# Two transformer stacks on one core: attention scores of several heads interleaved on TensorE

## The reference

```python
s = jnp.einsum('bnqkgd,bnjkd->bnkgqj', qb, kband).astype(jnp.float32) * (d ** -0.5)      # B
m = jnp.maximum(s.max(axis=-1, keepdims=True), sink)
p = jnp.exp(s - m)
denom = p.sum(axis=-1, keepdims=True) + jnp.exp(sink - m)
o = jnp.einsum('bnkgqj,bnjkd->bnqkgd', (p / denom).astype(v.dtype), vband)
...
s = jnp.einsum('bqhcd,bkhcd->bhcqk', qq, k).astype(jnp.float32) * scale                  # C
a = (p[:, :, 0] - lam * p[:, :, 1]).astype(v.dtype)
...
q = jnp.concatenate([q[..., :MLA_NOPE], rope(q[..., MLA_NOPE:], positions)], -1) * (dqk ** -0.5)
k = jnp.concatenate([k_nope, jnp.broadcast_to(k_pe, (B, S, H, MLA_ROPE))], -1)           # MLA
s = jnp.einsum('bhqd,bkhd->bhqk', qi, k, preferred_element_type=jnp.float32)
```

## Time and profile before

| | |
|---|---|
| median of 3 runs | 2145.54 us (2145.14 to 2146.28) |
| profiled execution | 2144.2 us, its span 2142.0 us |
| mean granted TensorE clock | 0.998 |
| VectorE busy, ScalarE busy | 65%, 49% |
| chain that ended last | PE 91%, DVE 4% of the span |
| DMA | 377.95 MB, 176 GB/s on average |

### The profile page before, as it was taken

How to read it: one execution, slowest core, us unless ns; L and a number is a source line. 1 busy time by engine, 2 the same in 40 slices (tenths; PEclk the granted TensorE clock), 3 DMA queues, 4 the chain that set the end, 5 groups by cost and what they waited for, 6 DMA issues and landing times.

```text
span 2142.0 us, 31461 instructions
## 1 busy us (share of the span) xinstructions
PE 2104.0 (98%) x13601; PEld 1902.0 (89%) x13607; DVE 1393.6 (65%) x1480; ACT 1059.8 (49%) x1240; POOL 142.1 (7%) x80
## 2 busy tenths in 40 slices
PE   7999999999999999999999999999999999999998
PEld 6998899899989989888998988998789989888997
DVE  5868777785867666566645786556775566566554
ACT  4655555555555544454544665445554443454442
POOL 2001110020101004000000000000000005000000
PEclk9999999999999999999999999999999999999999
DMA  7534565473355555555655645655356555455653
GB/s 250 179 113 137 192 204 179 162 226 119 133 179 181 189 185 179 172 172 177 199 186 171 202 167 187 204 189 146 128 172 209 187 185 193 157 174 171 207 190 106
DMA packets 252930, 377.95 MB, mean 176 GB/s; under 512 B 14085, under 2 KB 195578, under 8 KB 252794
## 3 DMA queue, kind: packets, MB, share of 16 engines
q1 hardware_dynamic: 252506, 374.90, 53.4%
q10 hardware_dynamic: 288, 1.05, 0.1%
HBM read 374.87 MB, written 1.05 MB: 175 GB/s over the span
## 4 chain that ended last, share of the span: by engine, by line
PE 91%; DVE 4%; DVEq 1%; ACT 1%; DMA 1%; issue 0%; POOL 0%; SPq 0%; POOLq 0%; ACTq 0%
PE bank L733 46%; PE acc L733 42%; PE bank L731 2%; DVE slot_lo L1866 2%; DVEq L1861 1%; DMA slot<-in_w_in 1%; PE acc L731 0%; POOL arena L2638 0%; DVE arena L2216 0%; ACT slot_hi L1412 0%; ACT arena L1407 0%; DVE arena L2472 0%; SPq L595 0%; DVE arena L1368 0%; ACT arena L1603 0%
## 5 line engine op out<-in xcount | busy, mean ns | idle before, releaser
L1866 DVE TENSOR_TENSOR slot_lo<-slot,slot_hi 128x2048 fp32r<-128x2048 f32 (+1 forms) x344 | 804.4, 2345 | 347.6 <-ACT slot_hi L1412 346.8
L733 PE MATMUL bank<-split,slot_hi 128*128 128x256 f32 x4508 | 818.8, 284 | 1.0 <-ACT arena L1407 1.0
L1412 ACT ACTIVATE slot_hi<-slot 128x2048 fp32r<-128x2048 f32 (+1 forms) x344 | 652.2, 1902 | 254.3 <-DMA slot<-in_mlp_w 136.4
L733 PEld LDWEIGHTS bank<-split,slot_hi 128*128 128x128 f32 x4508 | 707.9, 192 | 9.5 <-issue 3.8
L733 PE MATMUL acc<-slot_hi,split 128*128 128x512 f32 (+1 forms) x2116 | 667.9, 389 | 10.1 <-DVE split L2389 3.3
L733 PE MATMUL bank<-split,slot_lo 128*128 128x256 f32 x2254 | 638.3, 283 | 0.0
L733 PEld LDWEIGHTS acc<-slot_hi,split 128*128 128x128 f32 x2116 | 396.4, 188 | 92.4 <-issue 9.9
L733 PEld LDWEIGHTS bank<-split,slot_lo 128*128 128x128 f32 x2254 | 432.5, 192 | 0.0
L733 PE MATMUL acc<-slot_lo,split 128*128 128x512 f32 (+1 forms) x1058 | 410.0, 388 | 0.0
L733 PEld LDWEIGHTS acc<-slot_lo,split 128*128 128x128 f32 x1058 | 199.7, 189 | 36.4
L1407 ACT ACTIVATE arena<-bank 128x512 f32<-128x512 f32 (+2 forms) x143 | 81.2, 577 | 282.3 <-PE bank L733 270.8
(11 more groups left out here) (228 smaller groups left out, 1370.0 us busy)
## 6 DMA issues: line engine op xcount, KB each, us to landing
slot<-in_mlp_w SPq DMA_DIRECT2D x128, 1024.0 KB, 5.3
slot<-in_ret_w_in SPq DMA_DIRECT2D x48, 1024.0 KB, 5.2
slot<-in_w_up SPq DMA_DIRECT2D x40, 1024.0 KB, 5.1
slot<-in_w_in SPq DMA_DIRECT2D x38, 1024.0 KB, 5.3
slot<-in_w_down SPq DMA_DIRECT2D x22, 1024.0 KB, 4.9
slot<-in_ret_w_o SPq DMA_DIRECT2D x16, 1024.0 KB, 4.9
slot<-in_lru_w_in SPq DMA_DIRECT2D x10, 1024.0 KB, 5.3
slot<-in_w_out SPq DMA_DIRECT2D x8, 1024.0 KB, 5.1
```

Of the source, the lines that this page charges most:

```text
L733: i = nc.tensor.matmul(o, w, m, start=start, stop=stop)
L1412: A(whi[u.r][:, 0:u.cols], raw[u.r][:, 0:u.cols], ACT.Copy).then_inc(slot_hi[u.r], 1)
L1866: TTO(wlo[u.r][:, 0:u.cols], raw[u.r][:, 0:u.cols], f32(whi[u.r][:, 0:u.cols]), ALU.subtract)\
```

## The change

`softmax_scores` gets a parameter `by`: it opens the banks of `by` heads at once and makes, for each tile and each product of `pairs`, that product for all of these heads in turn. A and B run by two, C and MLA by four. The position of a banded head (`window_head`) becomes 0, 4, 1, 5 in the first group and 2, 6, 3, 7 in the second, so that neighbours lie in different halves and belong to different key/value heads. What depends on that order follows: the value columns, the view of the sinks, and where `values` writes each head (two multiplications of 128 elements in place of one of 256, for each tile of groups 1 and 2).

```diff
--- before.py
+++ after.py
@@ -948,17 +948,18 @@
 
             pe.wait_ge(V["ident_loaded"], 16)
 
-            def softmax_scores(name, ms, pairs):
-
-
-                for m in ms:
-                    o, end = open_bank(banks[name, m])
-                    ab = pairs(m)
+            def softmax_scores(name, ms, pairs, by=1):
+
+                for g in range(0, len(ms), by):
+                    opened = [open_bank(banks[name, m]) for m in ms[g:g + by]]
                     for tt in range(TT):
                         c0, n = tt * P, (tt + 1) * P
-                        for i, (q, k) in enumerate(ab):
-                            mm(o[:, c0:c0 + n], q[:, tt * P:(tt + 1) * P], k[:, 0:n], i == 0, i == len(ab) - 1,
-                               end if tt == 1 and i == len(ab) - 1 else None)
+                        for i in range(len(pairs(ms[0]))):
+                            for m, (o, end) in zip(ms[g:g + by], opened):
+                                ab = pairs(m)
+                                q, k = ab[i]
+                                mm(o[:, c0:c0 + n], q[:, tt * P:(tt + 1) * P], k[:, 0:n], i == 0, i == len(ab) - 1,
+                                   end if tt == 1 and i == len(ab) - 1 else None)
 
             def prob_transposes(name, u, src):
 
@@ -998,12 +999,15 @@
                     for n in ns:
                         two_tiles(slots[f"w_in{L}", 9 + n], banks[f"g{L}", n])
 
+                def window_head(i):
+                    return 4 * (i % 2) + i // 2
+
                 def pairs(m):
                     if m < 4:
                         p, q, k = 64 * (m % 2), m // 2, 2 + m // 2
                         n = 64
                     elif m < 12:
-                        h = m - 4
+                        h = window_head(m - 4)
                         p, q, k = 64 * (h // 4), 4 + h % 4, 8
                         n = 64
                     else:
@@ -1030,7 +1034,7 @@
                             if g == 0:
                                 c = V1A + j * HD
                             elif g < 3:
-                                c = V1B + (g - 1) * HD
+                                c = V1B + (j % 2) * HD
                             else:
                                 c = V1C + ((g - 3) * 2 + j) * HD
                             weighted(o[:, (tt * nh + j) * HD:(tt * nh + j + 1) * HD], pt1[:, g % 2, j, :],
@@ -1052,17 +1056,17 @@
                     mm_t.then_inc(end, 1)
                 gates([3])
                 in_sbuf(f"qk{L}", range(7))
-                softmax_scores(f"s{L}", range(4), pairs)
+                softmax_scores(f"s{L}", range(4), pairs, 2)
                 gates([4, 5])
-                softmax_scores(f"s{L}", range(4, 8), pairs)
+                softmax_scores(f"s{L}", range(4, 8), pairs, 2)
                 probs(0, [0, 1, 2, 3], 0)
                 gates([6, 7])
-                softmax_scores(f"s{L}", range(8, 12), pairs)
+                softmax_scores(f"s{L}", range(8, 12), pairs, 2)
                 probs(1, [4, 5, 6, 7], 4)
                 gates([8, 9])
-                softmax_scores(f"s{L}", range(12, 16), pairs)
+                softmax_scores(f"s{L}", range(12, 16), pairs, 4)
                 probs(2, [8, 9, 10, 11], 8)
-                softmax_scores(f"s{L}", range(16, 20), pairs)
+                softmax_scores(f"s{L}", range(16, 20), pairs, 4)
                 gates([10])
                 probs(3, [12, 13], 12)
                 in_sbuf(f"y{L}", range(3))
@@ -1305,10 +1309,10 @@
             wait(V["rot_out"], 10)
             in_sbuf("mq", range(4))
             in_sbuf("mkv", range(2))
-            softmax_scores("ms", range(4), mla_pairs)
+            softmax_scores("ms", range(4), mla_pairs, 4)
             wait(V["rot_out"], 11)
             in_sbuf("mkv", range(2, 4))
-            softmax_scores("ms", range(4, 8), mla_pairs)
+            softmax_scores("ms", range(4, 8), mla_pairs, 4)
             mla_values(0)
             mla_values(1)
             mla_transposes(0)
@@ -1931,6 +1935,9 @@
                 if n == 3:
                     dve.drain().then_inc(V["tab_free"], 1)
 
+            def by_value(a):
+                return a.rearrange("p (c v) -> p c v", v=2)
+
             def masked_max(name, ms, sc, g, mask, scale, maxed, sink=None):
                 for j, m in enumerate(ms):
                     u = banks[name, m]
@@ -1946,12 +1953,12 @@
                     TS(sm(g, 0), sm(g, 0), scale, None, ALU.mult)
                     d()
                     for tt in range(TT):
-                        TTO(sm(g, 0, tt), sm(g, 0, tt), sink, ALU.max)
+                        TTO(by_value(sm(g, 0, tt)), by_value(sm(g, 0, tt)), sink, ALU.max)
                     d()
                     TS(sm(g, 1), sm(g, 0), -1.0, None, ALU.mult)
                     d()
-                    TTO(sm(g, 5, 0), sink, sm(g, 1, 0), ALU.add)
-                    TTO(sm(g, 5, 1), sink, sm(g, 1, 1), ALU.add).then_inc(V[maxed], 1)
+                    TTO(by_value(sm(g, 5, 0)), sink, by_value(sm(g, 1, 0)), ALU.add)
+                    TTO(by_value(sm(g, 5, 1)), sink, by_value(sm(g, 1, 1)), ALU.add).then_inc(V[maxed], 1)
 
             def lo_hidden(h, r):
 
@@ -2062,7 +2069,8 @@
                 gate_split(5)
 
                 def scores(g):
-                    sink = tokc[:, T_SINK + 4 * (g - 1):T_SINK + 4 * g] if g in (1, 2) else None
+                    sink = (tokc[:, T_SINK:T_SINK + 8].rearrange("p (v g c) -> p g c v", v=2, g=2)[:, g - 1, :, :]
+                            if g in (1, 2) else None)
                     masked_max(f"s{L}", range(4 * g, 4 * g + 4), sc1, g, band if g in (1, 2) else causal,
                                (HD if g < 3 else 32) ** -0.5, "scores_max", sink)
 
@@ -2099,9 +2107,15 @@
                         r = sm(g, 4, tt)
                         if g >= 3:
                             r = r.rearrange("p (h c) -> p h c", c=2)[:, :, 0]
-                        last = TTO(y1[:, tt, c:c + nh * HD].rearrange("p (h n) -> p h n", n=HD),
-                                   bank[u.r][:, tt * nh * HD:(tt + 1) * nh * HD].rearrange("p (h n) -> p h n", n=HD),
-                                   spread(r, nh, HD), ALU.mult)
+                        o = y1[:, tt, c:c + nh * HD].rearrange("p (h n) -> p h n", n=HD)
+                        y = bank[u.r][:, tt * nh * HD:(tt + 1) * nh * HD].rearrange("p (h n) -> p h n", n=HD)
+                        if g in (1, 2):
+                            for v in range(2):
+                                b = y1[:, tt, 256 + 256 * v + 128 * (g - 1):256 + 256 * v + 128 * g]
+                                last = TTO(b.rearrange("p (h n) -> p h n", n=HD), y[:, v:4:2, :],
+                                           spread(r, nh, HD)[:, v:4:2, :], ALU.mult)
+                        else:
+                            last = TTO(o, y, spread(r, nh, HD), ALU.mult)
                     last.then_inc(bank_read[u.r], 1)
 
                 scores(0)
```

## The result

| | before | changed |
|---|---|---|
| median | 2145.9 us (2145.14 to 2146.28) | 2131.76 us (2129.68 to 2136.55), 4 runs |
| profiled execution, its span | 2144.2, 2142.0 us | 2129.68, 2127.9 us |
| mean granted TensorE clock of it | 0.998 | 0.999 |

The ratio is 0.9938, with a 95% interval of [0.992, 0.9955]: 13.3 us less (the medians differ by 14.1), where 12.2 were forecast. The same kernel came in two later jobs at 0.9949 [0.9934, 0.9964] and 0.9952 [0.9938, 0.9965], that is 10.9 and 10.3 us less. The forecast of 2133.3 (2130.8 to 2137.5) holds.

What follows compares the result with a forecast made beforehand. TensorE, busy 98% of the span, was taken as the bound. Gains 0.2 (A) + 5.2 (banded) + 0 (C) + 6.8 (latent, less its wait) = 12.2 us, from 2145.54 to 2133.3 us; range 2130.8 to 2137.5.

Steps and rivals of the forecast that it cites:

- The bound: Whole kernel: TensorE's matmuls are busy 98% of the span, so microseconds taken from TensorE count.
- (1) Branch A: Branch A's scores by two: halves already overlap, 1.62 to 1.52 us, 0.2 us over two layers.
- (2) Banded groups: Branch B's scores: mixing row halves makes a group like A, 2.81 to 1.52 us, 5.2 us over four groups.
- (3) Branch C: Differential heads by four: all four row quarters overlap already in 0.89 us, so gain 0.
- (4) Latent scores: MLA scores by four: fewer height changes and paired 64-row products, 16.71 to 9.42 us, 7.3 us saved.
- the price of a change of height: Latent scores: switching between 128-row and 64-row passes costs 0.195 us each; a group of four drops from sixteen to four.
- the complete pairing of the 64-row products: Latent scores: neighbouring 64-row products in alternating halves overlap, 1.31 us a group; without it the stage saves 4.7 us.
- Rival (a): Latent scores: the 64-row products don't pair, gain 2.6 us less, 2135.5 us; chance 0.12 together with a late VectorE.
- The new wait: Before the latent weighted sums: TensorE waits 0.45 us for VectorE's softmax chain, leaving 6.8 us gain; ends 0 and 2 us.
- Layers keep the gain: Rest of each layer: VectorE's chain moves with TensorE, extra value multiplications are covered; cost 0, otherwise under 0.8 us per layer.
- Rival (c): Layers: the banded gain is given back at a VectorE chain or an unmoved weight, 2138.5 us; chance 0.05.
- Rival (e): TensorE's granted clock falls through the half-filled array or clustered waits; 35 us at half clock gives 2150.8 us; chance 0.02.

Runs made afterwards that it cites:

- run 2: Kernel before with only the banded heads' order changed, nothing interleaved, latent heads as before: 2138.18 us, ratio 0.9971 to the kernel before.
- run 5: Changed kernel with the latent scores taken by two heads instead of four: 2132.98 us, one run.
- run 1: Changed kernel again, no edit, timed beside the kernel before: 2131.88 us, ratio 0.9949.
- run 4: Kernel before with only the latent scores taken by four, branches A, B and C as before: 2137.88 us, ratio 0.9974 to the kernel before.
- run 7: Changed kernel with 24 empty drains added at the start of VectorE's program: 2130.48 us, one run.
- run 8: Changed kernel with two VectorE weight splits moved behind the latent probability copies, first values and divisors: 2130.02 us, ratio 0.9937 to the kernel before.
- run 9: Changed kernel again, unaltered, timed in the same job as run 10: 2134.05 us, ratio 0.9952 to the kernel before.
- run 10: Kernel of run 8 (later weight splits) again, timed beside run 9: 2127.11 us, ratio 0.9922 to the kernel before.
- run 3: Kernel before with only A and B interleaved by two, C by four; banded order and latent heads old: 2143.9 us, ratio 1.0002 to the kernel before.
- run 6: Changed kernel with the 64-row products of each latent four in head order 0, 2, 1, 3: 2131.58 us, one run.

## Why the prediction was right

- **The bound**. What was taken from TensorE arrived at the end: 12.0 us of stages less their wait, 11.9 of span in the pair of executions with one clock drop each (12.4 at VectorE's last instruction).
- **(1) Branch A**: 1.51, forecast 1.52. **(2) Banded groups**: 1.51, forecast 1.52; 5.2 us in four groups as forecast. The ground for it was that A's two heads start at 95.79 and 95.80; run 2 shows that this is the cause, as the order alone gives B exactly A's former time.
- **(3) Branch C**: forecast 0, measured 0.02 a group, 0.08 in all. That is inside what the sum left open.
- **(4) Latent scores**: 9.34, forecast 9.42; the saving 7.37, forecast 7.3. Both parts hold: the price of a change of height (0.195 forecast; 0.21 by the difference of runs 5 and 1, 0.185 if 12 heads' passes of 0.655 are taken off the 9.34) and the complete pairing of the 64-row products. Rival (a) had the second one wrong. (The quotient behind 0.655 is 0.657; it moves no sum by more than 0.03.)
- **The new wait** is the term that was mis-sized: 0.45 forecast, 0.92 measured. 0.57 of it is the chain itself (runs 4 and 7), 0.12 longer than its steps added up to. The other 0.35 come of the 0.43 us gap in VectorE's stream, which the eight additional instructions move to just this place. The prediction costed those instructions by their elements alone. That the sum still came so near is in part luck: the same shift takes away the gap at L2256 of the kernel before, which the prediction didn't have either, and gives 0.34 us back.
- **Layers keep the gain**: yes. The lead in front of the first group of C, 3.76, is 3.81 at 485 us, one whole layer end and MLP later. Rival (c) falls; the value multiplications, twice as many, delay nothing.
- **Rival (e)**: the half-filled array ran at 1.00 in all overlapping stages. The clock drop at 1255 (1261 before) comes in some executions and not in others, as the prediction left open. It begins around the end of the one wait of 2.9 us for a split, from 0.7 us before it (run 8) to 0.1 behind it (run 9); in the earlier trace rows too it began at 1261.00, 0.16 ahead of the end and not behind it. The changed kernel with it (run 1):

```profile
1255.62 0.77 PE L733 MATMUL acc<-slot_hi,split 128*128 128x512 f32 x1 [2.91 <-DVE slot_lo L1870]
```

The same instruction without it, in the first profile of the changed kernel:

```profile
1254.76 0.47 PE L733 MATMUL acc<-slot_hi,split 128*128 128x512 f32 x1 [2.91 <-DVE slot_lo L1870]
```

The wait is equal to the hundredth, the matmul takes 0.77 at 1.2 GHz and 0.47 at 2.4. What decides it is not shown. A drop of 3.4 us at half clock is 1.7 us lost, most of what separates the low runs of the kernel before (2142.3 to 2143.9) from the high ones (2144.8 to 2147.3); of the nine beside runs 9 and 10 the low ones had a mean clock of 0.998 to 0.999, the high ones of 0.997 to 0.998. So the median shown for it at first, 2145.54, was one of high runs only, and the medians of later jobs lay between 2143.53 and 2145.68.

A smaller form of (e) did come. Of the 13 executions of the changed kernel four have a mean clock of 0.995 and take 2134.96 to 2136.55 us; the other nine take 2129.68 to 2134.05. None of the 37 executions of the kernel before whose clock is on record is below 0.997, and none of the 37 of runs 2 to 8 and 10; that is hardly chance. It is the likely reason why the ratios of runs 1 and 9 come to 10.9 and 10.3 us and the profiles to 12.0. No execution at 0.995 was profiled, so where its clock fell is not shown.

## What to carry to other kernels

In these runs fp32 products that use half or a quarter of the rows overlap when a product in other rows follows soon in the program, and whether it follows directly matters little. So look first for groups whose members all lie in the same rows: there is something to gain by mixing them, and little by interleaving a group that is mixed already. Where products of different heights alternate, sort them by height: each change cost 0.2 us, twice the 0.11 us of a 128-column pass. Sorting makes the results of a group arrive together and late, so look behind the stage for other work (here a weight split of 2.3 us) that stands in the chain TensorE now waits for, and move it: that gave another 3.0 us.

## What was not expected of the hardware

- A gap of 0.43 us on VectorE that nothing released, at a fixed position of its instruction stream: eight instructions more put it into the chain, 24 empty ones took it out again (0.35 us of TensorE's time). The kernel before had such a gap in another chain, worth 0.34 us, and the same eight instructions took that one away. So in this kernel an edit of VectorE's program can gain or lose some 0.3 us without touching the work.
- The granted clock fell not only behind the wait at 1255 but also in the latent part. In run 2 it was half for 6.8 us from 1531.11, in the middle of the idle 1.86 us (to 1532.14) at the transposes of the second group; in run 5 for 3.4 us from 1527.24, 0.36 behind the same wait. TensorE's timeline in run 2, where a group of four transposes takes 1.12 us and at the full clock six take 0.88:

```profile
1532.14 1.12 PE L731 MATMUL bank<-con,arena 128*128 128x128 f32 x4 [1.86 <-DVE arena L2577]
```

The same wait left the clock at 1.00 in the kernel before and in the changed one. Runs 8 and 10 are without it, and none of their eight executions has a clock of 0.995, where the changed kernel had four in 13; eight are too few to tell that from chance.
- The start of branch A, with the same instructions ahead of it, scatters between 94.7 and 96.4 us over the twelve profiles.
